# Four seven-product units of eight in the feed-forward input of a macaron trunk, in alternating order

## The chip, the cores and the metric

One core of a Trainium2 chip runs the whole program. The metric is the device time of one execution in microseconds (us). The engines named here: TensorE (PE) with its weight loads (PEld), VectorE (DVE), ScalarE (ACT), GpSimd (POOL), and SyncE (SP), which issues the loads of the weights.

## The reference

A layer of depth one on 256 tokens of width 2048: a SwiGLU block at half weight, an mLSTM mixer, a second SwiGLU block, a final norm.

```python
def swiglu_ffn(x, g, w_in, w_out):
    a, b = jnp.split(rmsnorm(x, g) @ w_in, 2, axis=-1)
    return (jax.nn.silu(a) * b) @ w_out

h = h + 0.5 * swiglu_ffn(h, ffn_norm[0, 0], ffn_w_in[0, 0], ffn_w_out[0, 0])
u = rmsnorm(h, mix_norm[0])
h = h + mlstm_mixer(u, a_w_in[0], a_b_if[0], a_head_norm[0], a_w_out[0])
h = h + 0.5 * swiglu_ffn(h, ffn_norm[0, 1], ffn_w_in[0, 1], ffn_w_out[0, 1])
return rmsnorm(h, final_norm)
```

All arrays are float32; w_in is 2048 x 11264, w_out 5632 x 2048.

## The kernel before

**Precision.** Every wide product is made of three TensorE matmuls of rounded operands: high x high, high x low, low x high. ScalarE writes the high part of a weight tile (a copy into the rounded type), VectorE the low part (raw minus high). So each weight passes through both engines before TensorE reads it. `product` (lines 486 to 490) is one such triple on one 128x512 tile, here called a product.

**The feed-forward input.** The output columns of w_in come in 11 pairs of 512-column tiles, a (left, for silu) and b (right). The first pair is computed the plain way by `run` (line 426). The other ten, `GROUPS` = 10, go through units. A unit takes one pair of k tiles, k and k + 8, and both column tiles: a 2x2 block of weights against a 2x2 block of inputs (two token tiles T0 and T1, two k). Done plainly that is 8 products (`plain_unit`); with sums of inputs (`s_hi`, `s_lo`) and sums of weights (`mixed`) it is 7, after Strassen and Winograd (`seven_unit`). There are 8 units in a group; `UNITS` gives the order plain, seven, plain, seven, plain, seven, plain, plain. The eight products of a plain unit go to the banks p2, p4, p5 and p3, those of a seven unit to p1 to p7. A plain unit uses differences of the inputs (`d_hi`, `d_lo`) for p3.

**Items and slots.** The high and low weights lie in 3 slots each. A plain unit fills one slot (an item), in two halves; a seven unit two: the straight item (three of the raw tiles) and the mixed item (four sums). So a group has 11 items, and item n lies in slot n mod 3. `free` makes ScalarE wait until TensorE has used the item three before (`pair_used`). Raw weights have 3 slots of their own, one for a unit; `load_groups` on the SP queue issues two loads for a unit when the unit three before has been read.

**Queues.** The order on each engine is written out by hand. For one group:

- TensorE: `plain_unit` or `seven_unit` in the order of `UNITS`; after units 1 and 2 `turn_hidden` transposes the hidden tile of the group before.
- ScalarE (`ffn_in` of the scalar block): `high_plain`, `high_straight`, `high_mixed` halves; `silu` of the group before; `keep_hidden` twice; `keep_first`, which copies p1 into `sums`.
- VectorE (`ffn_in` of the vector block): for a seven unit `mix_weights` (three instructions, the later ones waiting for the earlier), `low_straight`, `low_mixed` twice; for a plain unit `low_plain` twice; and the drains of the banks, `drain_products` (p6, p7), `drain_left` (p2, p4), `drain_right` (p5), `drain_last` (p3), then `gate_hidden`.

**The boundary of groups.** The first unit is plain. Its first four products write p2 and p4 and wait for `drain_left` of the group before (`drained`, all but two); the next four write p5 and p3 and wait for all five drains. VectorE does `drain_products` between the two halves of the next group's unit 0, and the other drains behind `mix_weights` and `low_straight` of its unit 1.

**Lines.** 426 matmuls of `run`; 483 hidden transposes; 488 to 490 `product`; 750 and 1139 high and low parts outside the units; 825, 834 and 843 ScalarE's high parts of plain halves, straight and mixed items; 1221, 1229 and 1238 VectorE's low parts of the same; 1253, 1256 and 1258 `mix_weights`; 1266 and 1268 `drain_products`; 1275, 1282 and 1289 left, right and last drain; 1211 `gate_hidden`; 1201 `gate_first`; 1400 `low_hidden`.

Of the kernel before, what the change touches and what calls it, by code (L numbers as in the profile page):

```python
# [5 lines left out]
F32 = mybir.dt.float32  # L6
# [6 lines left out]
P = 128  # L13
# [3 lines left out]
RING = 4  # L17
EPS = 1e-6
UNITS = (("plain", 3), ("seven", 0), ("plain", 4), ("seven", 1), ("plain", 5), ("seven", 2),
         ("plain", 6), ("plain", 7))  # L20
SEVENS, PLAINS = 3, 5
FIRST_ITEM = (0, 1, 3, 4, 6, 7, 9, 10)
ITEMS = 11
# [4 lines left out]
def trunk_program(nc, x, ffn_norm, ffn_w_in, ffn_w_out, mix_norm, a_w_in, a_b_if, a_head_norm,  # L28
# [54 lines left out]
    with ExitStack() as ctx:  # L83
# [16 lines left out]
        gain_rows = sb("gain_rows", [3 * KD, P])  # L100
        first_rows = sb("first_rows", [KD, P])
# [40 lines left out]
        with ExitStack() as side_place:  # L142
            def sp_(name, shape, dt=F32):
                return side_place.enter_context(nc.sbuf_tensor(name, shape, dt))

            sp_("side_pad", [P, KF, SEQ])
            d_sum = sp_("d_sum", [P, 2, PLAINS, P])
            sp_("side_pad2", [P, 25 * SEQ])
            u_all = sp_("u_all", [P, KD, SEQ])
            s_sum = sp_("s_sum", [P, 4, SEVENS, P])  # L150
# [8 lines left out]
        with ExitStack() as gate_place:  # L159
# [7 lines left out]
            select = gp("select", [HEADS, HEADS, P], F32R)  # L167
        with ExitStack() as end_place:
# [3 lines left out]
        ctx.enter_context(nc.sbuf_tensor("place_fence", [P, 98, SEQ], F32))  # L172
# [244 lines left out]
        def _(pe):  # L417
# [76 lines left out]
            def plain_unit(i, group, u, k):  # L494
# [3 lines left out]
                first, last = u == 0, u == len(UNITS) - 1  # L498
                done = DRAINS * (GROUPS * i + group)
                if first and group:  # L500
                    pe.wait_ge(drained, done - 2)
                elif first:
                    pe.wait_ge(silu_ready, SILUS[i] + 1)
                pe.wait_ge(pair_low, halves(i, n) + 1)
                for b, kk in enumerate((k, k + HALF_K)):
                    for bank, tok in ((p2, T0), (p4, T1)):
                        mm = product(bank, u_hi[:, kk, tok], u_lo[:, kk, tok], hi[:, b], lo[:, b],
                                     first and b == 0, last and b == 1)
                mm.then_inc(pair_used, 1)
                if first and group:  # L510
                    pe.wait_ge(drained, done)
                elif first and i == 0:
                    pe.wait_ge(gains_ready, 2)
                pe.wait_ge(pair_low, halves(i, n) + 2)
                for b, kk in enumerate((k, k + HALF_K)):
                    mm = product(p5, u_hi[:, kk, T1], u_lo[:, kk, T1], hi[:, 2 + b], lo[:, 2 + b],
                                 first and b == 0, last and b == 1)
                if last:
                    mm.then_inc(right_summed, 1)
                for b in range(2):  # L520
                    mm = product(p3, d_hi[:, b, k - SEVENS], d_lo[:, b, k - SEVENS], hi[:, 2 + b],
                                 lo[:, 2 + b], first and b == 0, last and b == 1)
                mm.then_inc(pair_used, 1)

            def seven_unit(i, group, u, k):
# [3 lines left out]
                first, last = k == 0, k == SEVENS - 1  # L529
                pe.wait_ge(pair_low, halves(i, n) + 2)  # L530
                product(p1, u_hi[:, k, T0], u_lo[:, k, T0], hi[:, 0], lo[:, 0], first, last)
                product(p2, u_hi[:, k + HALF_K, T0], u_lo[:, k + HALF_K, T0], hi[:, 1], lo[:, 1],
                        False, False).then_inc(pair_used, 1)
                product(p3, s_hi[:, 3, k], s_lo[:, 3, k], hi[:, 2], lo[:, 2], False, False)\
                    .then_inc(pair_used, 1)
                hi, lo = hi_slots[(n + 1) % SLOTS], lo_slots[(n + 1) % SLOTS]
                if first and group == 0:
                    pe.wait_ge(tile_ready, R_HID[i] - R_HID1 + 1)
                pe.wait_ge(pair_low, halves(i, n + 1) + 1)
                product(p5, s_hi[:, 0, k], s_lo[:, 0, k], hi[:, 0], lo[:, 0], False, False)  # L540
                product(p7, s_hi[:, 2, k], s_lo[:, 2, k], hi[:, 1], lo[:, 1], first, last)\
                    .then_inc(pair_used, 1)
                pe.wait_ge(pair_low, halves(i, n + 1) + 2)
                product(p6, s_hi[:, 1, k], s_lo[:, 1, k], hi[:, 2], lo[:, 2], first, last)
                product(p4, u_hi[:, k + HALF_K, T1], u_lo[:, k + HALF_K, T1], hi[:, 3], lo[:, 3],
                        False, False).then_inc(pair_used, 1)

            def ffn_in_rest(i):
# [4 lines left out]
                for group in range(GROUPS):  # L553
                    for u, (kind, k) in enumerate(UNITS):
# [4 lines left out]
                        if u == 1 or u == 2:  # L559
                            turn_hidden(i, group, u - 1)  # L560
# [181 lines left out]
        def _(act):  # L742
# [94 lines left out]
            def high_mixed(i, group, u, half):  # L837

                n, s = item(group, u) + 1, SEVENS * (GROUPS * i + group) + UNITS[u][1]
                act.wait_ge(mixed_ready, 3 * s + (3 if half else 1))  # L840
                free(i, n, half)
                at = slice(2 * half, 2 * half + 2)
                nc.scalar.activation(hi_slots[n % SLOTS][:, at], mixed[:, at], ACT.Copy)\  # L843
# [9 lines left out]
            def keep_first(i, group):  # L853

                act.wait_ge(pair_used, halves(i, item(group, 5)) + 1)
# [14 lines left out]
            def ffn_in(i):  # L870
# [10 lines left out]
                for group in range(GROUPS):  # L881
                    if group == 0:
                        high_plain(i, group, 0, 0)
                        high_plain(i, group, 0, 1)
                    high_straight(i, group, 1)
                    high_mixed(i, group, 1, 0)
                    if group:
                        silu(i, group - 1)
                    high_mixed(i, group, 1, 1)
                    high_plain(i, group, 2, 0)  # L890
                    high_plain(i, group, 2, 1)
                    high_straight(i, group, 3)
                    keep_hidden(i, group, 0)
                    high_mixed(i, group, 3, 0)
                    high_mixed(i, group, 3, 1)
                    high_plain(i, group, 4, 0)
                    high_plain(i, group, 4, 1)
                    keep_hidden(i, group, 1)
                    high_straight(i, group, 5)
                    high_mixed(i, group, 5, 0)  # L900
                    high_mixed(i, group, 5, 1)
                    high_plain(i, group, 6, 0)
                    high_plain(i, group, 6, 1)
                    keep_first(i, group)
                    high_plain(i, group, 7, 0)
                    high_plain(i, group, 7, 1)
                    if group < GROUPS - 1:
                        high_plain(i, group + 1, 0, 0)
# [769 lines left out]
```

## Time and profile before

| | us |
|---|---|
| median of 3 runs | 1840.58 (1840.19 to 1841.08) |
| the profiled execution | 1839.55 |
| its span, first to last instruction | 1837.5 |
| PE busy in the span | 1820.7 (99%), 8228 matmuls |
| DVE busy | 1314.6 (72%) |
| ACT busy | 938.8 (51%) |
| HBM read | 347.24 MB, 190 GB/s over the span |

A busy time is the time in which an engine had an instruction in work, so for TensorE, whose matmuls overlap, it says little more than that it did not wait. The distance between the starts of two instructions is what one costs in a full queue. "Idle before" and the arrow behind it give how long the engine stood still and what released it.

### The profile page before, as it was taken

What the parts mean: (1) busy time and instruction counts of PE and PEld (TensorE: products, weight loads), DVE (VectorE), ACT (ScalarE), POOL (GpSimd) and SP (SyncE); (2) the same over time, 40 slices, a digit from 0 to 9 for tenths busy, and PEclk for the clock granted to TensorE, in tenths of its full rate; (3) what the DMA queues carried; (4) which work ended last, traced back from release to release, by engine and by line L of the source; (5) the groups of instructions that cost most, each with busy time, mean ns of one, the idle gap of its engine ahead of it and who ended that gap; (6) DMA issues with size and microseconds to landing.
All of it is one profiled execution on the core that took longest, in us unless ns stands there. A gap on an engine that the chain in (4) does not pass through costs nothing.

```text
span 1837.5 us, 21636 instructions
## 1 busy us (share of the span) xinstructions
PE 1820.7 (99%) x8228; PEld 1506.1 (82%) x8228; DVE 1314.6 (72%) x1470; ACT 938.8 (51%) x1040; POOL 38.2 (2%) x52
## 2 busy tenths in 40 slices
PE   8999999999999999999999999999999999999998
PEld 6888888888888888888888888888888888888886
DVE  7888888888855554555477757888888888754444
ACT  6555555555654444444445445555555555653442
POOL 0000000000100000000000000000000000000000
PEclk9999999999999999999999999999999999999999
DMA  7666555665556565557645456666665566556664
GB/s 230 222 210 206 196 197 184 197 200 199 178 182 200 190 191 182 166 169 206 192 140 149 160 183 190 211 207 207 204 202 187 184 205 202 194 188 198 194 193 137
DMA packets 180607, 350.68 MB, mean 191 GB/s; under 512 B 10848, under 2 KB 11040, under 8 KB 180256
## 3 DMA queue, kind: packets, MB, share of 16 engines
q1 hardware_dynamic: 179952, 348.17, 59.3%
q0 software_dynamic: 432, 1.18, 0.3%
q8 instruction: 63, 1.03, 0.2%
q14 instruction: 32, 0.26, 0.0%
q10 hardware_dynamic: 128, 0.03, 0.0%
HBM read 347.24 MB, written 2.10 MB: 190 GB/s over the span
## 4 chain that ended last, share of the span: by engine, by line
PE 98%; DVE 1%; ACT 1%; issue 0%; DMA 0%; DVEq 0%; ACTq 0%
PE acc L426 49%; PE acc L490 8%; PE acc L488 8%; PE acc L489 8%; PE aux L490 7%; PE aux L488 7%; PE aux L489 7%; PE aux L483 1%; PE aux L455 1%; PE aux L699 1%; PE aux L649 0%; PE aux L687 0%; DMA h<-in_x_dram 0%; ACT sums L787 0%; ACT u_hi L765 0%
## 5 line engine op out<-in xcount | busy, mean ns | idle before, releaser
L1139 DVE TENSOR_TENSOR w_lo<-raw,w_hi 128x1024 fp32r<-128x1024 f32 x336 | 410.8, 1228 | 330.0 <-ACT w_hi L750 327.5
L750 ACT ACTIVATE w_hi<-raw 128x1024 fp32r<-128x1024 f32 x336 | 354.4, 1059 | 349.7 <-PE acc L426 339.7
L426 PE MATMUL acc<-w_hi,g_hi 128*128 128x512 f32 x704 | 274.9, 390 | 0.0
L426 PE MATMUL acc<-w_hi,g_lo 128*128 128x512 f32 x704 | 274.0, 389 | 0.0
L426 PE MATMUL acc<-w_lo,g_hi 128*128 128x512 f32 x704 | 273.9, 389 | 0.0
L426 PE MATMUL acc<-w_hi,u_hi 128*128 128x512 f32 x512 | 203.9, 398 | 2.8 <-DVE w_lo L1139 2.8
L426 PE MATMUL acc<-w_hi,u_lo 128*128 128x512 f32 x512 | 200.2, 391 | 0.0
L426 PE MATMUL acc<-w_lo,u_hi 128*128 128x512 f32 x512 | 200.2, 391 | 0.0
L1221 DVE TENSOR_TENSOR w_lo<-raw,w_hi 128x1024 fp32r<-128x1024 f32 x112 | 135.2, 1222 | 51.2 <-ACT w_hi L825 51.2
L825 ACT ACTIVATE w_hi<-raw 128x1024 fp32r<-128x1024 f32 x112 | 116.4, 1057 | 87.1 <-PE aux L490 46.1
L426 PEld LDWEIGHTS acc<-w_hi,g_lo 128*128 128x128 f32 x704 | 132.1, 188 | 27.4
L426 PEld LDWEIGHTS acc<-w_lo,g_hi 128*128 128x128 f32 x704 | 132.2, 188 | 27.2
L426 PEld LDWEIGHTS acc<-w_hi,g_hi 128*128 128x128 f32 x704 | 132.2, 188 | 27.3
L488 PE MATMUL acc<-w_hi,u_hi 128*128 128x512 f32 x358 | 140.7, 393 | 0.0
L490 PE MATMUL acc<-w_hi,u_lo 128*128 128x512 f32 x358 | 139.6, 390 | 0.0
L489 PE MATMUL acc<-w_lo,u_hi 128*128 128x512 f32 x358 | 139.4, 389 | 0.0
L426 PEld LDWEIGHTS acc<-w_hi,u_hi 128*128 128x128 f32 x512 | 96.6, 189 | 22.6 <-issue 2.8
L426 PEld LDWEIGHTS acc<-w_hi,u_lo 128*128 128x128 f32 x512 | 96.5, 189 | 20.6
L426 PEld LDWEIGHTS acc<-w_lo,u_hi 128*128 128x128 f32 x512 | 96.7, 189 | 18.9
L1238 DVE TENSOR_TENSOR w_lo<-mixed,w_hi 128x1024 fp32r<-128x1024 f32 x72 | 85.7, 1218 | 1.8 <-ACT w_hi L843 0.2
L843 ACT ACTIVATE w_hi<-mixed 128x1024 fp32r<-128x1024 f32 x72 | 74.5, 1053 | 17.9 <-PE acc L490 17.9
L834 ACT ACTIVATE w_hi<-raw 128x1536 fp32r<-128x1536 f32 x28 | 41.8, 1491 | 75.6 <-PE aux L490 66.8
(227 smaller groups left out, 3231.6 us busy)
## 6 DMA issues: line engine op xcount, KB each, us to landing
raw<-in_ffn_w_in_dram SPq DMA_DIRECT2D x248, 512.0 KB, 4.5
raw<-in_ffn_w_out_dram SPq DMA_DIRECT2D x176, 512.0 KB, 4.6
raw_more<-in_ffn_w_in_dram SPq DMA_DIRECT2D x104, 512.0 KB, 4.5
raw<-in_a_w_in_dram SPq DMA_DIRECT2D x96, 512.0 KB, 4.3
raw<-in_a_w_out_dram SPq DMA_DIRECT2D x32, 512.0 KB, 4.5
h<-in_x_dram SPq DMA_DIRECT2D x4, 512.0 KB, 8.8
final_gain<-in_final_norm_dram POOLq DMA_DIRECT2D x1, 1024.0 KB, 5.3
out_dram<-h SPq DMA_DIRECT2D x1, 1024.0 KB, 3.9
```

Source lines behind the costliest of these rows:

```text
L426: mm = nc.tensor.matmul(acc[:, TT * (c % 2) + t, :], s[:, k, tok], w[:, ring, kk, :], start=(k == 0 and n == 0), stop=(k == GK * granules ...
L455: mm = nc.tensor.transpose(ps[:, at:at + P], block_, ident[:, :])
L488: nc.tensor.matmul(bank, side_hi, wide_hi, start=start, stop=False)
L489: nc.tensor.matmul(bank, side_hi, wide_lo, start=False, stop=False)
L490: return nc.tensor.matmul(bank, side_lo, wide_hi, start=False, stop=stop)
L750: nc.scalar.activation(w_hi[:, n % RING], raw[:, n % RING], ACT.Copy)\
L825: nc.scalar.activation(hi_slots[n % SLOTS][:, at], raw_slots[unit % SLOTS][:, at], ACT.Copy)\
L834: nc.scalar.activation(hi_slots[n % SLOTS][:, 0:3], raw_slots[unit % SLOTS][:, 0:3], ACT.Copy)\
L843: nc.scalar.activation(hi_slots[n % SLOTS][:, at], mixed[:, at], ACT.Copy)\
L1139: nc.vector.tensor_tensor(w_lo[:, n % RING], raw[:, n % RING], w_hi[:, n % RING].bitcast(F32), ALU.subtract)\
L1221: nc.vector.tensor_tensor(lo_slots[n % SLOTS][:, at], raw_slots[unit % SLOTS][:, at], hi_slots[n % SLOTS][:, at].bitcast(F32), ALU.subtract)\
L1238: nc.vector.tensor_tensor(lo_slots[n % SLOTS][:, at], mixed[:, at], hi_slots[n % SLOTS][:, at].bitcast(F32), ALU.subtract)\
```

## The change

Four of the eight k pairs become seven-product units, and the order alternates: seven, plain, seven, plain, and so on. A group has 12 items instead of 11. The first unit of a group is now a seven unit, and its third product (p3) waits for all five drains of the group before. The mixed item is no longer halved in 2 + 2 tiles but in 3 + 1 (`low_mixed`, `low_added`). `drain_products` moves behind `low_straight` of the next group's unit 0. The sums of weights stay on VectorE. The two tiles of raw gains get another place in memory, to make room for the wider `s` tiles.

```diff
-UNITS = (("plain", 3), ("seven", 0), ("plain", 4), ("seven", 1), ("plain", 5), ("seven", 2),
-         ("plain", 6), ("plain", 7))
-SEVENS, PLAINS = 3, 5
-FIRST_ITEM = (0, 1, 3, 4, 6, 7, 9, 10)
-ITEMS = 11
+UNITS = (("seven", 0), ("plain", 4), ("seven", 1), ("plain", 5),
+         ("seven", 2), ("plain", 6), ("seven", 3), ("plain", 7))
+SEVENS, PLAINS = 4, 4
+FIRST_ITEM = (0, 2, 3, 5, 6, 8, 9, 11)
+ITEMS = 12
...
             def seven_unit(i, group, u, k):
...
+                done = DRAINS * (GROUPS * i + group)
+                if first and group:
+                    pe.wait_ge(first_kept, GROUPS * i + group)
+                elif first:
+                    pe.wait_ge(silu_ready, SILUS[i] + 1)
                 pe.wait_ge(pair_low, halves(i, n) + 2)
                 product(p1, u_hi[:, k, T0], u_lo[:, k, T0], hi[:, 0], lo[:, 0], first, last)
+                if first and group:
+                    pe.wait_ge(drained, done - 2)
                 product(p2, u_hi[:, k + HALF_K, T0], u_lo[:, k + HALF_K, T0], hi[:, 1], lo[:, 1],
-                        False, False).then_inc(pair_used, 1)
+                        first, False).then_inc(pair_used, 1)
+                if first and group:
+                    pe.wait_ge(drained, done)
...
+                product(p3, s_hi[:, 3, k], s_lo[:, 3, k], hi[:, 2], lo[:, 2], first, False)\
                     .then_inc(pair_used, 1)
                 hi, lo = hi_slots[(n + 1) % SLOTS], lo_slots[(n + 1) % SLOTS]
+                pe.wait_ge(pair_low, halves(i, n + 1) + 1)
+                product(p5, s_hi[:, 0, k], s_lo[:, 0, k], hi[:, 0], lo[:, 0], first, False)
...
+                product(p7, s_hi[:, 2, k], s_lo[:, 2, k], hi[:, 1], lo[:, 1], first, last)
+                product(p6, s_hi[:, 1, k], s_lo[:, 1, k], hi[:, 2], lo[:, 2], first, last)\
                     .then_inc(pair_used, 1)
                 pe.wait_ge(pair_low, halves(i, n + 1) + 2)
                 product(p4, u_hi[:, k + HALF_K, T1], u_lo[:, k + HALF_K, T1], hi[:, 3], lo[:, 3],
-                        False, False).then_inc(pair_used, 1)
+                        first, False).then_inc(pair_used, 1)
...
-                        if u == 1 or u == 2:
-                            turn_hidden(i, group, u - 1)
+                        if u == 1 or u == 3:
+                            turn_hidden(i, group, u // 2)
...
+            def high_mixed(i, group, u):
...
+                act.wait_ge(mixed_ready, 3 * s + 2)
+                free(i, n, 0 if n >= SLOTS else 1)
+                nc.scalar.activation(hi_slots[n % SLOTS][:, 0:3], mixed[:, 0:3], ACT.Copy)\
+                    .then_inc(pair_high, 1)
+
+            def high_added(i, group, u):
...
+                act.wait_ge(mixed_ready, 3 * s + 3)
+                free(i, n, 1)
+                nc.scalar.activation(hi_slots[n % SLOTS][:, 3], mixed[:, 3], ACT.Copy)\
                     .then_inc(pair_high, 1)
...
                 for group in range(GROUPS):
...
+                    high_straight(i, group, 0)
+                    high_mixed(i, group, 0)
+                    high_added(i, group, 0)
                     if group:
                         silu(i, group - 1)
...
+                    high_plain(i, group, 1, 0)
+                    high_plain(i, group, 1, 1)
...
+                    high_plain(i, group, 5, 0)
                     keep_hidden(i, group, 1)
...
+                    high_plain(i, group, 5, 1)
...
                     high_plain(i, group, 7, 0)
                     high_plain(i, group, 7, 1)
...
+                    keep_first(i, group)
...
             def drain_products(i, group):
...
-                dve.wait_ge(pair_used, halves(i, item(group, 5) + 2))
+                dve.wait_ge(pair_used, halves(i, item(group, 6) + 2) - 1)
...
                 for group in range(GROUPS):
...
+                    mix_weights(i, group, 0)
+                    low_straight(i, group, 0)
                     if group:
+                        drain_products(i, group - 1)
+                        low_mixed(i, group, 0)
                         drain_left(i, group - 1)
...
                         drain_right(i, group - 1)
                         drain_last(i, group - 1)
...
+                        low_added(i, group, 0)
                         gate_hidden(i, group - 1)
                     else:
                         gate_first(i)
...
+                        low_mixed(i, group, 0)
+                        low_added(i, group, 0)
+                    low_plain(i, group, 1)
...
+                    mix_weights(i, group, 6)
+                    low_straight(i, group, 6)
+                    low_mixed(i, group, 6)
+                    low_added(i, group, 6)
+                    low_plain(i, group, 7)
+                drain_products(i, GROUPS - 1)
```

## Rows read from the trace of the kernel before

**Rows 1.** The page, part 1: busy time (share of the span) and instructions.
```profile
PE 1820.7 (99%) x8228; PEld 1506.1 (82%) x8228; DVE 1314.6 (72%) x1470; ACT 938.8 (51%) x1040; POOL 38.2 (2%) x52
```

**Rows 2.** Busy time by stretch: the stage in block one, and one group.
```profile
core 0: us, PE busy (x) PEld busy (x) DVE busy (x) ACT busy (x) POOL busy (x), PEclk, DMA share, GB/s
58.95:483.42 424.47, 424.47 (x1911) 351.35 (x1910) 368.90 (x350) 239.69 (x243) 0.00 (x0) 1.00 0.60 199
101.18:143.62 42.44, 42.44 (x192) 35.14 (x191) 36.99 (x36) 23.68 (x25) 0.00 (x0) 1.00 0.60 199
```

**Rows 3.** Waits of TensorE, whole run: us in total, times, longest us.
```profile
PE acc L426 <- DVE w_lo L1139: 2.8, 2, 2.4
```

**Rows 4.** The chain that ended last: start us, us, what.
```profile
495.42 54.45 PE acc L426 x240
```

**Rows 5.** Timeline of VectorE: start us, us, engine, line, operation, out<-in.
```profile
134.76 0.68 DVE L1266 TENSOR_TENSOR sums<-acc,sums 128x512 f32<-128x512 f32 x1
135.48 0.69 DVE L1268 TENSOR_TENSOR sums<-acc,sums 128x512 f32<-128x512 f32 x1
136.08 1.22 DVE L1221 TENSOR_TENSOR w_lo<-raw,w_hi 128x1024 fp32r<-128x1024 f32 x1
...
140.28 1.76 DVE L1229 TENSOR_TENSOR w_lo_more<-raw_more,w_hi_more 128x1536 fp32r<-128x1536 f32 x1 [0.40 <-ACT w_hi_more L834]
141.96 1.22 DVE L1275 TENSOR_TENSOR tile<-acc,sums 128x1024 f32<-128x1024 f32 x1
143.09 1.21 DVE L1238 TENSOR_TENSOR w_lo<-mixed,w_hi 128x1024 fp32r<-128x1024 f32 x1
144.23 1.21 DVE L1282 TENSOR_TENSOR sums<-aux,sums 128x1024 f32<-128x1024 f32 x1
145.54 0.69 DVE L1289 TENSOR_TENSOR sums<-aux,sums 128x512 f32<-128x512 f32 x1
146.15 1.22 DVE L1238 TENSOR_TENSOR w_lo<-mixed,w_hi 128x1024 fp32r<-128x1024 f32 x1
147.28 1.41 DVE L1211 SCALAR_TENSOR_TENSOR tile<-sums,rstd,tile 128x512 f32<-128x512 f32 x2
148.61 1.22 DVE L1221 TENSOR_TENSOR w_lo<-raw,w_hi 128x1024 fp32r<-128x1024 f32 x1
...
151.78 1.22 DVE L1253 TENSOR_TENSOR mixed<-raw 128x1024 f32<-128x1024 f32 x1
...
154.37 1.75 DVE L1229 TENSOR_TENSOR w_lo_more<-raw,w_hi_more 128x1536 fp32r<-128x1536 f32 x1
```

**Rows 6.** The page, part 6: loads, number, KB each, median us to landing.
```profile
raw<-in_ffn_w_in_dram SPq DMA_DIRECT2D x248, 512.0 KB, 4.5
```

**Rows 7.** Timeline of three engines at one handover.
```profile
106.61 0.39 PE L490 MATMUL aux<-w_hi_more,d_lo 128*128 128x512 f32 x1
...
107.10 1.06 ACT L825 ACTIVATE w_hi_more<-raw 128x1024 fp32r<-128x1024 f32 x1 [1.66 <-PE aux L490]
...
108.19 1.23 DVE L1221 TENSOR_TENSOR w_lo_more<-raw,w_hi_more 128x1024 fp32r<-128x1024 f32 x1 [0.81 <-ACT w_hi_more L825]
```

**Rows 8.** The chain, and TensorE's timeline, where it waited once.
```profile
35.76 1.24 DVE w_lo L1139
...
37.04 0.50 PE L426 MATMUL acc<-w_hi,u_hi 128*128 128x512 f32 x1 [0.40 <-DVE w_lo L1139]
...
37.38 0.40 PE L426 MATMUL acc<-w_lo,u_hi 128*128 128x512 f32 x1
```

**Rows 9.** Timeline of ScalarE: item 1 of the first group.
```profile
59.23 1.49 ACT L834 ACTIVATE w_hi<-raw 128x1536 fp32r<-128x1536 f32 x1 [4.40 <-PE acc L426]
```

**Rows 10.** Timeline of VectorE at the end of the stage, block one.
```profile
480.90 1.23 DVE L1275 TENSOR_TENSOR tile<-acc,sums 128x1024 f32<-128x1024 f32 x1 [0.40 <-PE acc L490]
...
487.37 1.41 DVE L1211 SCALAR_TENSOR_TENSOR tile<-sums,rstd,tile 128x512 f32<-128x512 f32 x2
```

**Rows 11.** Timeline of TensorE at the start of the kernel.
```profile
12.12 0.63 PE L426 MATMUL acc<-w_hi,u_lo 128*128 128x512 f32 x1
12.55 0.63 PE L426 MATMUL acc<-w_hi,u_hi 128*128 128x512 f32 x1
```

## What the change does to the time

> **What bounds the kernel now.** I read the page's busy shares first: TensorE is busy 99% of the span [rows 1]. That view alone can mislead, so next the waits with TensorE as the waiting engine: in the whole run it waits for VectorE twice, 2.8 us together, none of it in the stage that changes [rows 3]. So this is a TensorE-bound kernel, and its time is a count of matmuls times their pitch, 54.45/240 = 0.2269 us [rows 4]. The changed stage runs from 58.95 to 483.42 us and again in the second feed-forward block; there one group takes 42.44 us and in it VectorE is busy 36.99 us [rows 2]. That second number is what to look at: the cover under which the other engines work is 5.45 us per group. The group's 183 matmuls take 41.52 us, its two blocks of transposes the remaining 0.92.
>
> **What is removed.** A plain unit has 8 products of 3 matmuls, a seven-product unit 7. One unit in each of 20 groups changes kind: 60 matmuls x 0.2269 = 13.6 us. If TensorE never waited, a group would take 180 x 0.2269 + 0.92 = 41.76 us.
>
> **What VectorE gets.** I cost its instructions by start-to-start distance where nothing was waited for [rows 5]: a 1024-wide subtraction 1.14 us (143.09 to 144.23), a 1536-wide one 1.68 (140.28 to 141.96), a 512-wide step 0.61 (145.54 to 146.15), the three sums of `mix_weights` together 2.59 (151.78 to 154.37), the two of `drain_products` 1.32 (134.76 to 136.08), a 1024-wide drain whose successor waits for it 1.31 (144.23 to 145.54), `gate_hidden` 1.33 (147.28 to 148.61). After the change a group has 8 plain halves (9.12), 4 x 2.59 of sums (10.36), 8 of the 1536-wide (13.44), 4 of the 512-wide (2.44) and the drains (1.32 + 1.31 + 1.31 + 0.61 + 1.33 = 5.88): 41.24 us against 41.76. The cover is down to half a microsecond, so any wait of VectorE that cannot be made up shows. The loads are not in play: they carry the same bytes and land 4.5 us after their issue [rows 6], and each slot is refilled some ten microseconds before its unit is read. Moving the two gain tiles costs no instruction. ScalarE keeps over a third of its time free and matters only as a link in a chain.
>
> **Where the order decides.** Let X be the time since a group began, for a TensorE that does not stall; a product is 0.68 us. Items end at: 0 at 2.04, 1 at 4.76, 2 at 10.20 (then transposes), 3 at 12.71, 4 at 15.43, 5 at 20.88 (transposes), 6 at 23.39, 7 at 26.11, 8 at 31.56, 9 at 33.60, 10 at 36.32, 11 at 41.76. A slot is refilled when TensorE has used the item three before. How long such a handover takes is in [rows 7]: the last matmul of a half starts at 106.61, so its slot ends at 106.84; ScalarE starts at 107.10, VectorE at 108.19: 0.26, then 1.09.
> Now the new boundary. The next group's third product (into p3) waits for all five drains of the group before, and VectorE does the drains behind `mix_weights(0)`, `low_straight(0)`, `drain_products` and `low_mixed(0)`. It can't begin these before the second half of unit 7 (item 11), whose slot is free when item 8 is used: X = 31.56 + 0.26 + 1.09 = 32.91. I walked the queue up to there: by its own work VectorE would come to that half at about 32.0 (it waits once more, at unit 5, for ScalarE behind the hidden transposes, and still gets there first). Then 1.14 + 2.59 + 1.68 + 1.32 + 1.68 = 8.41, so `drain_left` starts at 41.32. Left, right and last take 1.31 + 1.31 + 0.69, and TensorE goes on 0.04 behind them: that step is 37.04 behind 35.76 + 1.24 in the chain; its next matmul comes 0.34 instead of 0.23 after, 0.11 more [rows 8]. Together 3.46: p3 effectively starts at 44.78. It was due at 41.76 + 1.36 = 43.12. Stall per boundary 1.66 us. In the steady state it is one loop: p3 to the end of item 8, 129 matmuls and two blocks of transposes, 30.20; handover 1.35; VectorE 8.41; drains and restart 3.46; sum 43.42 against 42.44 now. It does not grow, since every part hangs on the stalled TensorE again. There are 9 boundaries in each of two blocks: 18 x 1.66 = 29.9 us.
> p2, due at X = 42.44, waits for `drain_left` (42.54) a tenth of a microsecond, inside the same stall. `low_added(0)` and `gate_hidden` behind the drains are in time: their readers come 2.7 us and more after p3. Before, the first unit after a boundary was plain: four products on p2 and p4, 2.72 us long, covered the right and last drains; the new order has 1.36 us there.
>
> **Start of the stage.** Item 1 of group 0 takes a slot that is free only when the last granule is used; ScalarE starts there at 59.23 now [rows 9], for a unit that TensorE reads 5.44 us into the group. Now it is read at 2.04: 59.23 + 1.49 + 0.04, `low_mixed(0)` 1.75, restart 0.15 gives 62.65 against 58.95 + 2.04 = 60.99: 1.66 us. `gate_first` (59.2 to 60.6) hides under ScalarE's copy. The preparation of the sides gets 0.5 us longer (wider by a third, the differences narrower) in a part where VectorE has time. Twice: 3.3 us.
> **End of the stage.** `drain_products` waits for item 10's first half, X = 35.9; then `low_hidden(0)` behind its copy (37.7) and two splits put `drain_left` at 41.08, its end at 42.30, and TensorE, due at 41.76, goes on at 42.4: 0.7. The gate comes 6.47 after the left drain (487.37 after 480.90 [rows 10]) and ends at 48.96; the transposes are due after 24 matmuls at 47.9: 1.1. Twice 1.8 = 3.6 us.
>
> **Sum.** On the profiled execution, 1839.55 us: - 13.6 + 29.9 + 3.3 + 3.6 = + 23.2, so 1862.8. The median of the runs is 1.0 above the profiled one: 1863.8, and I say 1863.5, since part of the restart may overlap.
> Bounds. The restart at a stall is between 0.04 and 0.15: 2 us over 18. The 512-wide copy on ScalarE and 1536-wide instructions from `mixed` have no row, but have the same shapes' rows and stand off the loop or in it once at 1.68 +- 0.05. Start and end stalls together between 3 and 8 us. That gives 1857 to 1869 for the forecast's own case; nothing excludes small waits more per loop of 0.1 to 0.2, to 1872.
>
> **Rule against row.** TensorE runs at the full one of its levels (2.4 GHz) throughout this stage: granted 1.00 [rows 2]. At the start of the kernel, after idling, the matmuls come 0.43 us apart (12.12, 12.55), 1.2 GHz, for 8 matmuls [rows 11]. The idle of about 0.8 us before 37.04 was followed at once by the full pitch [rows 8]. No row here has a gap of 1.4 us in a busy stretch. The Trainium skill, "TensorE: Matmul & The Clock Gate", section "A second HAM failure mode: psum-queue depth-cycling", says that frequent small idles between groups can make the clock fall and rise again. By that rule the change would lose more than my sum; it is a rival below. No run here shows it yet.
>
> **Rivals.**
> (a) The cover holds, and the time falls. Mechanism: the drains reach p3 in time, that is `drain_left` starts by X = 39.8 instead of 41.32. Then only the matmuls count, and the start and end at their lower bound: 1840.6 - 13.6 + 3 = 1830, or 1827 with none. For it: VectorE's work, 41.24, does fit into 41.76, and at every other reader but this one my walk finds it in time by 0.3 us or more. Against: the handover through item 8 is fixed by TensorE itself and 8.41 us of VectorE's work stand behind it. It decides once that chain is 1.5 us shorter. Chance 0.07.
> (b) The wait at unit 7 is not the last, VectorE's own stream is: the half at 32.02 instead of 32.91, stall 0.77. Then 18 x 0.77 = 13.9, sum + 7.2: 1848. For it: a halving of the handover (the record of PE's ends is modelled). Against: [rows 7] repeats at every plain half. Chance 0.07, and another 0.04 for a mixture of (a) and (b) that ends within 3.7 us of 1840.6.
> (c) The clock falls at each boundary: 8 matmuls at 0.43 instead of 0.23 are 1.6 us, inside the loop, 18 times: + 29, 1892. Chance 0.04.
> (d) The forecast, 1850 to 1872: 0.78.
>
> **Numbers.** A measurement of this kernel can tell about 0.2% (3.7 us) from no change. Faster 0.07 (a); same 0.04; slower 0.89 (forecast, b, c). The range goes from 1847, which takes in (b), to 1872; outside are (a), the mixture and (c), 0.15.
>
> **What would show it.** In the profile after: 8168 matmuls, 60 fewer than the 8228 of now [rows 1]; the waits list gets a new line, TensorE for VectorE's `drain_last` (L490 or L488 on aux, 18 times, about 1.5 us each) and a smaller one for `drain_left`; one group takes 43.4 us; VectorE is busy about 41 us of it, with one wait of 0.9 us for ScalarE before unit 7's second half and one of about 1.3 before unit 5's. The granted clock stays 1.00. I am wrong if `drain_left` starts more than 1.9 us before a group ends, if TensorE waits at another place than p3, or if the distance of groups is under 42.4.

## The result, and the profile after

| | us |
|---|---|
| median after, 4 runs | 1864.87 (1863.99 to 1865.23) |
| before, beside them | 1840.83 |
| ratio, 95% interval | 1.0131 [1.0115, 1.0147] |
| profiled execution after, its span | 1865.09, 1863.0 |
| predicted | 1863.5 (1847 to 1872) |

The kernel became 24 us slower. The 1840.83 is the median of four executions beside it, three of them from 1840.19 to 1841.08 and one, far outside, at 5542.8 us. The page, part 1, against [rows 1]:

```profile
PE 1819.7 (98%) x8168; PEld 1492.3 (80%) x8168; DVE 1391.6 (75%) x1550; ACT 965.2 (52%) x1060; POOL 37.5 (2%) x52
```

The 60 matmuls are gone, but TensorE's busy time fell by 1.0 us and not by 13.6. A record of a matmul lasts 0.39 us at a pitch of 0.23, so the first 0.16 us of each stall counts as busy, and a delay shorter than that does wholly. The busy line hides the loss; the view to read is the waits of TensorE (engine, line, what it waited for: us in total, times, longest us), against [rows 3]:

```profile
PE aux L489 <- DVE sums L1304: 20.9, 18, 1.2
...
PE acc L427 <- DVE w_lo L1146: 2.8, 2, 2.4
PE aux L489 <- DVE w_lo L1245: 2.8, 2, 1.4
PE aux L484 <- DVE tile L1218: 1.8, 2, 0.9
...
PE acc L427 <- DVE tile L1290: 0.9, 2, 0.4
```

The old line (2.8, two times) is still there. New are one wait for `drain_last` (L1304) at each of the 18 boundaries (1.16 us of idle each, where the prediction had said about 1.5), two for `low_mixed` (L1245) at the starts of the stage, and two each for the gate (L1218) and the left drain (L1290) at its ends. The smaller wait for `drain_left`, p2's, is too short for the list of TensorE (0.13 us, all of it counted as busy). The list of the weight loads (PEld) has it, beside the same 18 for `drain_last`:

```profile
PEld aux L489 <- DVE sums L1304: 28.7, 18, 1.6
...
PEld acc L489 <- DVE tile L1290: 7.1, 18, 0.4
```

One group, from left drain to left drain, by stretch (columns as in [rows 2]; there 42.44 us with VectorE busy 36.99):

```profile
189.97:233.45 43.48, 42.32 (x189) 34.41 (x188) 40.76 (x40) 25.06 (x25) 0.00 (x0) 1.00 0.59 194
```

One boundary, VectorE's timeline from the second half of unit 7 on (start us, us, engine, line, operation, out<-in, idle before and what ended it):

```profile
225.06 1.23 DVE L1229 TENSOR_TENSOR w_lo_more<-raw,w_hi_more 128x1024 fp32r<-128x1024 f32 x1 [0.92 <-ACT w_hi_more L828]
...
231.79 1.75 DVE L1245 TENSOR_TENSOR w_lo<-mixed,w_hi 128x1536 fp32r<-128x1536 f32 x1
233.45 1.22 DVE L1290 TENSOR_TENSOR tile<-acc,sums 128x1024 f32<-128x1024 f32 x1
234.77 1.23 DVE L1297 TENSOR_TENSOR sums<-aux,sums 128x1024 f32<-128x1024 f32 x1
236.10 0.69 DVE L1304 TENSOR_TENSOR sums<-aux,sums 128x512 f32<-128x512 f32 x1
```

and TensorE's at the same boundary, p1's first matmul, p2's first, p2's last, p3's first:

```profile
233.91 0.39 PE L489 MATMUL aux<-w_hi,u_hi 128*128 128x512 f32 x1
...
234.72 0.50 PE L489 MATMUL acc<-w_hi,u_hi 128*128 128x512 f32 x1
...
235.30 0.39 PE L491 MATMUL acc<-w_hi,u_lo 128*128 128x512 f32 x1
236.85 0.50 PE L489 MATMUL aux<-w_hi,s_hi 128*128 128x512 f32 x1 [1.16 <-DVE sums L1304]
```

The chain can be read off: VectorE waits 0.92 us for ScalarE, whose slot TensorE has only just given back; then it never pauses until `drain_last`, and TensorE starts p3 0.06 us behind that.

### The profile page after: what moved, and what is told of

Read it like the earlier page. It is cut to its first block, busy times and chain, and to the rows that moved or that the text cites. A ratio compares the mean times of both kernels' runs of the same rounds, so it can differ in the third digit from the quotient of the medians.

```text
span 1863.0 us, 21675 instructions
## 1 busy us (share of the span) xinstructions
PE 1819.7 (98%) x8168; PEld 1492.3 (80%) x8168; DVE 1391.6 (75%) x1550; ACT 965.2 (52%) x1060; POOL 37.5 (2%) x52
## 4 chain that ended last, share of the span: by engine, by line
PE 84%; DVE 10%; issue 4%; ACT 2%; DMA 0%; DVEq 0%; ACTq 0%
PE acc L427 48%; PE acc L489 6%; PE acc L491 6%; PE acc L490 6%; PE aux L489 5%; PE aux L491 5%; PE aux L490 5%; DVE w_lo L1237 2%; DVE sums L1297 1%; DVE tile L1290 1%; DVE mixed L1268 1%; PE aux L484 1%; ACT w_hi_more L828 1%; PE aux L456 1%; DVE sums L1304 1%
## 5 line engine op out<-in xcount | busy, mean ns | idle before, releaser
L1146 DVE TENSOR_TENSOR w_lo<-raw,w_hi 128x1024 fp32r<-128x1024 f32 x336 | 410.6, 1228 | 325.0 <-ACT w_hi L753 322.6
L427 PE MATMUL acc<-w_hi,u_hi 128*128 128x512 f32 x512 | 204.1, 399 | 2.8 <-DVE w_lo L1146 2.8
L427 PE MATMUL acc<-w_hi,u_lo 128*128 128x512 f32 x512 | 200.6, 392 | 0.0
L427 PE MATMUL acc<-w_lo,u_hi 128*128 128x512 f32 x512 | 200.4, 391 | 0.0
L845 ACT ACTIVATE w_hi<-mixed 128x1536 fp32r<-128x1536 f32 x80 | 119.4, 1492 | 138.1 <-DVE mixed L1271 130.4
L1229 DVE TENSOR_TENSOR w_lo_more<-raw,w_hi_more 128x1024 fp32r<-128x1024 f32 x108 | 129.6, 1220 | 28.4 <-ACT w_hi_more L828 28.4
L1245 DVE TENSOR_TENSOR w_lo<-mixed,w_hi 128x1536 fp32r<-128x1536 f32 x80 | 140.0, 1750 | 0.3 <-ACT w_hi L845 0.3
L489 PE MATMUL acc<-w_hi_more,u_hi 128*128 128x512 f32 x320 | 124.5, 389 | 0.0
L490 PE MATMUL acc<-w_lo_more,u_hi 128*128 128x512 f32 x320 | 124.5, 389 | 0.0
L491 PE MATMUL acc<-w_hi_more,u_lo 128*128 128x512 f32 x320 | 124.5, 389 | 0.0
```

The costliest lines, as they stand in the source:

```text
L427: mm = nc.tensor.matmul(acc[:, TT * (c % 2) + t, :], s[:, k, tok], w[:, ring, kk, :], start=(k == 0 and n == 0), stop=(k == GK * granules ...
L489: nc.tensor.matmul(bank, side_hi, wide_hi, start=start, stop=False)
L490: nc.tensor.matmul(bank, side_hi, wide_lo, start=False, stop=False)
L491: return nc.tensor.matmul(bank, side_lo, wide_hi, start=False, stop=stop)
L845: nc.scalar.activation(hi_slots[n % SLOTS][:, 0:3], mixed[:, 0:3], ACT.Copy)\
L1146: nc.vector.tensor_tensor(w_lo[:, n % RING], raw[:, n % RING], w_hi[:, n % RING].bitcast(F32), ALU.subtract)\
```

## The experiments

All are variants of the kernel after, and the edits are shown against it. Each is timed beside the kernel before, whose median was 1839.85 us beside the first four (`extra_unit0` to `drains_first`) and 1840.10 beside the others. A "period" is the distance between two left drains in mid-stage: 42.44 before, 43.48 after, and 41.76 where TensorE never waits. A loop is what runs from one wait of TensorE to the next like it: TensorE's matmuls up to the one that frees a slot, the handover of that slot through ScalarE to VectorE, VectorE's queue up to the result that TensorE waits for, and TensorE's restart (the 0.15 us by which the next two matmuls come late).

**1. More work on the chain.** In groups 1 to 9, ahead of `low_straight` of unit 0, VectorE sums a raw tile into a spare column (declared beside the other tiles) that nobody reads:

```diff
+                if group and u == 0:
+                    nc.vector.tensor_reduce(spare[:, :], raw_slots[unit % SLOTS][:, 0], AXX, ALU.add)
                 nc.vector.tensor_tensor(lo_slots[n % SLOTS][:, 0:3], raw_slots[unit % SLOTS][:, 0:3],
```

> The changed kernel with one more VectorE instruction, a sum over a 128x512 tile whose result nobody reads, ahead of low_straight of unit 0, in 18 of the 20 groups. It stands between the wait for unit 7's second half and drain_left. My theory (a loop through that stretch of the queue, 43.5 us long): all of the instruction's length, about 0.6 us, is added to every group period, 18 x 0.6 = +11, so 1876 against 1864.9. Rival (VectorE's amount of work per group sets the period, wherever it stands): also about +11. This run alone tells nothing, its twin with the same instruction in unit 6 does.

Measured: 1880.14 us (1877.77 to 1881.45), ratio 1.0217 [1.0200, 1.0234]. The period is 44.07 behind all boundaries but 3, + 0.59 for 0.59 us of work: 18 x 0.59 = 10.6, and 1864.9 + 10.6 = 1875.5, as expected. The measured time is 4.6 us above that, which I had not expected. It lies at 3 of the 18 boundaries, where the period is 45.6. There TensorE's timeline, and below it two stretches, read:

```profile
104.55 0.50 PE L490 MATMUL acc<-w_hi,u_hi 128*128 128x512 f32 x1 [0.56 <-DVE tile L1293]
...
106.67 0.51 PE L490 MATMUL aux<-w_hi,s_hi 128*128 128x512 f32 x1 [1.15 <-DVE sums L1307]
107.00 0.60 PE L491 MATMUL aux<-w_lo,s_hi 128*128 128x512 f32 x1
107.40 0.63 PE L492 MATMUL aux<-w_hi,s_lo 128*128 128x512 f32 x1
107.83 0.63 PE L490 MATMUL aux<-w_hi,s_hi 128*128 128x512 f32 x1
```

```profile
104.00:108.00 4.00, 2.31 (x7) 1.59 (x8) 3.79 (x6) 3.23 (x4) 0.00 (x0) 0.88 0.19 74
108.00:112.00 4.00, 4.00 (x14) 3.18 (x13) 3.97 (x5) 1.49 (x1) 0.00 (x0) 0.70 0.04 6
```

Behind the two idles, 0.56 and 1.15 us, TensorE's matmuls come 0.43 us apart, the lower level, with a granted clock of 0.88 and 0.70 in the stretches, until 110.39. From 107.00 to there lie 8 matmuls in 3.39 us instead of 1.82: 1.6 us. That is rival (c) at its price; 3 x 1.6 = 4.7 makes up 1880. At the other 15 boundaries the same two idles left the clock at the full level, and in the kernel after (p2 0.13 late, then 1.16 of idle) it never fell: the granted clock is 1.00 in every 4 us of both stages.

**2. The same work off the chain,** ahead of unit 6 (`u == 6` in place of `u == 0`).

> The same additional instruction, the same number of times, ahead of low_straight of unit 6, where the trace of the changed kernel has VectorE waiting 0.92 us for ScalarE two units later. My theory: it shortens that wait to 0.3 us and costs nothing, 1864.9 within 1.5 us. Rival (the amount of work sets the period): +11, 1876, as in the twin.

Measured: 1864.98 us, ratio 1.0136 [1.0119, 1.0153]; period 43.49. It costs nothing. VectorE's timeline shows where it went, the wait ahead of unit 7's second half, 0.92 before:

```profile
219.00 0.68 DVE L1239 TENSOR_REDUCE spare<-raw 128x1 f32<-128x512 f32 x1
...
225.08 1.23 DVE L1230 TENSOR_TENSOR w_lo_more<-raw,w_hi_more 128x1024 fp32r<-128x1024 f32 x1 [0.33 <-ACT w_hi_more L829]
```

Runs 1 and 2 together: the time hangs on VectorE's work between that handover and `drain_last`, not on its amount in a group.

**3. The readers of the late banks moved back.** TensorE's products of unit 0 (in every group but the first) run in the order p1, p7, p6, p2, p4, p3, p5, those that need no late drain first, and `low_added(0)` goes up:

```diff
+                    pe.wait_ge(drained, done - 3)
...
+                    product(p7, s_hi[:, 2, k], s_lo[:, 2, k], hi_b[:, 1], lo_b[:, 1], True, False)
+                    product(p6, s_hi[:, 1, k], s_lo[:, 1, k], hi_b[:, 2], lo_b[:, 2], True, False)
+                    pe.wait_ge(drained, done - 2)
...
+                    pe.wait_ge(drained, done)
...
                         drain_left(i, group - 1)
+                        low_added(i, group, 0)
                         drain_right(i, group - 1)
                         drain_last(i, group - 1)
-                        low_added(i, group, 0)
```

> The changed kernel with the same work in another order at the boundary: TensorE's seven products of unit 0 run p1, p7, p6, p2, p4, p3, p5 (the two that need no drain of p2 to p5 come early), and VectorE does low_added(0) between drain_left and drain_right. p3 is then due 3.4 us after the boundary instead of 1.36. My theory: drain_last ends at X = 45.07 and p3 is due at 45.17, so the stall of 1.7 us goes, the period is 41.8 and the time 1864.9 - 18 x 1.7 = 1834, up to 1840 if single waits of 0.1 to 0.3 us remain. Rival (amount of work: VectorE needs 41.2 plus its waits of 2.2 us = 43.4): the period stays at 43.4 and the time within 3 us of 1865.

Measured: 1856.96 us (1856.73 to 1858.02), ratio 1.0095 [1.0078, 1.0111]: a miss. The period is 43.07. The wait for `drain_last` is gone, and another stands in its place:

```profile
PE acc L489 <- DVE w_lo_more L1248: 16.8, 18, 0.9
```

It is for `low_plain(1)`, the first half of item 2, next in VectorE's queue behind the drains and the gate. I had checked that reader only in a schedule in which TensorE is already late at p3, not at the period that I now hoped for. Its loop: from TensorE's start of item 2 (X = 4.76) to the end of item 8 (31.56) 26.80; handover 1.35; VectorE 8.41 up to `drain_left`, drains 3.23, `low_added` 0.61, gate 1.33, the half itself 1.22 and restart 0.15, together 14.95: 43.10 against 43.07. By the same walk it was there in the kernel after as well, 0.3 us shorter than the p3 loop of 43.42 and hidden by it.

**4. The drains first,** with TensorE's order left alone:

```diff
                         drain_products(i, group - 1)
-                        low_mixed(i, group, 0)
                         drain_left(i, group - 1)
                         drain_right(i, group - 1)
                         drain_last(i, group - 1)
+                        low_mixed(i, group, 0)
                         low_added(i, group, 0)
```

> The changed kernel with VectorE's order alone changed: low_mixed(0) behind drain_left, drain_right and drain_last instead of ahead of them. Then p3 is in time and p5, which reads the mixed item, is late. By my walk the loop is p5 to the end of item 8 29.52, handover 1.35, VectorE 6.73, left 1.31, right 1.31, last 0.61, low_mixed 1.75, restart 0.15: 42.73 instead of 43.42. That is 18 x 0.69 = -12.4, so 1852.5. Rival (amount of work): 1865. TensorE's wait should move from the drain's sum to the low part of the mixed item, about 1.0 us each.

Measured: 1862.46 us (1862.36 to 1862.85), ratio 1.0123 [1.0107, 1.0140]: a miss again, period 43.37. TensorE now waits for `low_mixed(0)` and, in its weight loads, again for the plain half:

```profile
PE aux L489 <- DVE w_lo L1245: 15.4, 20, 1.4
...
PEld acc L489 <- DVE w_lo_more L1229: 8.0, 18, 0.5
```

Item 2 has the same instructions ahead of it in any order, so its 43.1 remains; its first matmul starts right behind the end of its half in this run too (195.82 behind about 195.77). Of the 0.27 above 43.10, 0.23 is in VectorE's own queue, where `drain_left` now stands directly behind the drain whose sum it reads: 0.83 us from start to start, where the same instruction took 0.60 with another instruction behind it [rows 5].

```profile
186.86 0.69 DVE L1283 TENSOR_TENSOR sums<-acc,sums 128x512 f32<-128x512 f32 x1
187.69 1.23 DVE L1290 TENSOR_TENSOR tile<-acc,sums 128x1024 f32<-128x1024 f32 x1
```

**5. Run 3 with the gate behind item 2.** `gate_hidden` goes behind `low_plain(1)`. VectorE's part, with the edits of run 3 left in on TensorE's side and for `low_added`:

```diff
                         drain_last(i, group - 1)
-                        low_added(i, group, 0)
+                        low_plain(i, group, 1)
                         gate_hidden(i, group - 1)
```

> The run early_mixed came to 1857.0 with a period of 43.07 and a new wait of TensorE for the low part of plain unit 1 (item 2). New theory: p3 was only the first of several readers that VectorE reaches late; the loop through item 2 is TensorE from item 2 to the end of item 8, 26.80, handover 1.35, VectorE 14.94: 43.09. This kernel is early_mixed with gate_hidden moved behind low_plain(1), 1.33 us that item 2 need not wait for. Then item 3 (low_straight of unit 2) is the next late reader: 20.89 + 1.35 + 20.26 = 42.50, so 18 x 0.57 less: 1846.7, and TensorE's wait is at unit 2. Rival (VectorE's amount of work plus waits that don't move, 41.2 + 1.9): the same period 43.1 and 1857.

Measured: 1844.99 us (9 runs, 1844.35 to 1846.13), ratio 1.0027 [1.0017, 1.0037], period 42.40. As forecast, the next reader is late, the straight item of unit 2, whose loop I had walked at 42.50:

```profile
PE aux L489 <- DVE w_lo L1256: 5.8, 18, 0.3
```

So 20 of the 24 us lost come back by order alone, and still the kernel is not faster than before: with VectorE at about 41 us of work in 41.8, each reader has a loop that is a little too long.

**6. Less work on VectorE.** The third sum of each `mix_weights` goes to GpSimd:

```diff
-                dve.wait_ge(mixed_ready, 3 * s + 2)
-                nc.vector.tensor_tensor(mixed[:, 3], src[:, 1], mixed[:, 2], ALU.subtract)\
-                    .then_inc(mixed_ready, 1)
...
+                        pool.wait_ge(mixed_ready, 3 * s + 2)
+                        nc.gpsimd.tensor_tensor(mixed[:, 3], raw_slots[unit % SLOTS][:, 1], mixed[:, 2],
+                                                ALU.subtract).then_inc(mixed_ready, 1)
```

The loads into a raw slot wait for that sum too.

> The changed kernel with the third sum of each mix_weights (128x512, 0.61 to 0.72 us of VectorE) on GpSimd, which is idle in this stage; 4 per group, VectorE's work falls by 2.6 us per group. Loop theory: only the one between unit 7 and drain_left counts, the period goes from 43.48 to 42.8 and the time to 1852.5. Rival 1 (amount): the period is TensorE's own 41.8, 1834. Rival 2 (VectorE and GpSimd hold each other up at the memory): VectorE's instructions beside the sums grow from 1.75 to 2 us or more and the gain is under 6 us.

Measured: 1851.61 us (1851.55 to 1851.87), ratio 1.0063 [1.0046, 1.0080]; period 42.77, that is - 0.71, one sum, for the one sum of four that lies in the loop. Three more sums outside it bought nothing, as run 2 says they should. But VectorE is not 2.6 us freer, by the stretch of one group and by its timeline behind a sum of GpSimd's:

```profile
187.67:230.44 42.77, 42.08 (x189) 34.49 (x189) 41.29 (x37) 25.12 (x25) 10.96 (x4) 1.00 0.60 197
```

```profile
196.98 1.75 DVE L1251 TENSOR_TENSOR w_lo<-raw_more,w_hi 128x1536 fp32r<-128x1536 f32 x1
...
197.15 2.73 POOL L377 TENSOR_TENSOR mixed<-raw_more,mixed 128x512 f32<-128x512 f32 x1 [11.22 <-DVE mixed L1285]
198.65 2.85 DVE L1259 TENSOR_TENSOR w_lo<-mixed,w_hi 128x1536 fp32r<-128x1536 f32 x1
```

Its busy time is 41.29 with four sums fewer, since `low_mixed` beside GpSimd's sum takes 2.85 us instead of 1.75, in units 2, 4 and 6. So VectorE's busy time in a group rose by 0.53 us (40.76 to 41.29) while the period fell by 0.71: once more it isn't the amount of work that sets the period. For the same reason the run doesn't show what less work outside the loop would bring. The section on the hardware returns to this.

**7. The end of the stage alone.** VectorE's order there: one granule is split ahead of the left drain instead of two, the other drains and the gate before the last two:

```diff
                 low_hidden(i, 0)
-                split(g, 0, 2)
+                split(g, 0, 1)
                 drain_left(i, GROUPS - 1)
+                split(g, 1, 2)
                 low_hidden(i, 1)
-                split(g, 2, 3)
                 drain_right(i, GROUPS - 1)
                 drain_last(i, GROUPS - 1)
-                split(g, 3, 4)
                 gate_hidden(i, GROUPS - 1)
+                split(g, 2, 4)
```

> The changed kernel with the new order at the end of the stage alone: drain_left starts at X = 39.94 instead of 41.08, so TensorE finds it done; the gate ends at 46.7, before the transposes are due at 47.9; the third granule is late by 0.2 to 0.3 us. My theory (end term of 1.8 us per block): 3.0 us less, 1861.9. Rival (the end stall only hides another one right behind it): 1864.9 within 1 us.

Measured: 1861.73 us (1861.38 to 1862.23), ratio 1.0118 [1.0102, 1.0135], 3.1 below the kernel after. The waits for the left drain and the gate are gone; a short one for a split is left at each end. Its idle is 0.29 us and its delay 0.47, since that matmul comes 0.88 us behind the start of the transposes (499.28) where it came 0.41 behind it in the kernel after:

```profile
500.16 0.47 PE L427 MATMUL acc<-w_hi,g_hi 128*128 128x512 f32 x1 [0.29 <-DVE w_lo L1146]
```

**8. All three together:** the edits of runs 5, 6 and 7 in one kernel.

> early_late_gate with the third sums on GpSimd and with another order at the end of the stage (VectorE: drain_left ahead of the second granule, the drains and the gate ahead of the third and fourth). By the walk the loop through item 3 is then 42.50 - 2 x 0.7 = 41.1, shorter than TensorE's own 41.76, so no boundary stalls: 1864.9 - 18 x 1.72 - 3 = 1831. Rival (GpSimd's use of the memory slows VectorE): some of the waits stay, 1837 or more.

Measured: 1830.84 us (1830.36 to 1832.28), ratio 0.9951 [0.9934, 0.9967]. It beats both kernels, the one before by 9 us. Of TensorE's waits for VectorE, none is left at a boundary. The first row is the two old waits [rows 3] with the two short ones at the ends of the stage that run 7 left, and the second is the starts of the stage:

```profile
PE acc L441 <- DVE w_lo L1179: 3.4, 4, 2.4
PE aux L503 <- DVE w_lo L1278: 2.8, 2, 1.4
```

```profile
185.74:227.50 41.76, 41.76 (x189) 34.56 (x189) 41.08 (x36) 25.01 (x25) 10.95 (x4) 1.00 0.62 202
```

A group is TensorE's own 41.76 us, and the 34.0 us below the kernel after are 18 x 1.72 = 31.0 and about 3 from the ends. This is the time of rival (a), 1830, with the gain the change could have had.

## Why the prediction was right, and where it was not

The prediction was right in number and in mechanism: the loop that it named is the one that sets the period, and each of its four terms is seen in the trace. Wrong was the condition under which it let rival (a) come true. By term:

- **The matmuls.** 8168, and 41.76 us for a group without waits: run 8's stretch shows that number itself. Right.
- **The boundary.** Predicted was a loop of 43.42 with p3 1.66 us late. Measured: 43.48, 1.72 late, 18 x 1.72 = 31.0 against 29.9. From unit 7's half to `drain_left` it is 225.06 to 233.45, 8.39 against 8.41; left start to last end 3.34 (3.31); restart 0.06 and 0.11 (0.04 and 0.11). Run 1 shows that the loop carries added work one for one, run 2 that work ahead of the handover is free.
- **VectorE's waits** of 0.9 and about 1.3 for ScalarE: 0.92 as shown, and 1.28 ahead of unit 5's. VectorE is busy 40.76 us in a group, against "about 41". The 20 groups' waits of both kinds are one row of the waits:

```profile
DVE w_lo_more L1229 <- ACT w_hi_more L828: 45.2, 40, 1.8
```

- **Start of the stage.** TensorE goes on 1.75 us after the matmul before it instead of 0.23, and its next one is 0.11 late: 1.63 against 1.66. ScalarE starts the mixed item when TensorE gives the slot back, as forecast, and not when the sums are there: they are done at 58.05. No run undid this; it is read from the trace alone.

```profile
60.27 1.49 ACT L845 ACTIVATE w_hi<-mixed 128x1536 fp32r<-128x1536 f32 x1 [3.78 <-PE acc L427]
...
61.85 0.39 PE L491 MATMUL aux<-w_hi,s_lo 128*128 128x512 f32 x1
63.60 0.50 PE L489 MATMUL aux<-w_hi,s_hi 128*128 128x512 f32 x1 [1.37 <-DVE w_lo L1245]
```

- **End of the stage.** 495.40 instead of 494.81 and 0.11 behind: 0.7, as worked out. The transposes at 502.06 instead of 500.98: 1.1. Run 7 leaves a delay of 0.47 twice, so it should take 2.7 of these 3.6 away. The profiled executions differ by 3.7, and 1.0 of that lies at the start of the kernel, see the next point; the medians differ by 3.1.

```profile
494.58 0.39 PE L491 MATMUL aux<-w_hi_more,d_lo 128*128 128x512 f32 x1
495.40 0.50 PE L427 MATMUL acc<-w_hi,g_hi 128*128 128x512 f32 x1 [0.43 <-DVE tile L1290]
...
500.75 0.39 PE L427 MATMUL acc<-w_hi,g_lo 128*128 128x512 f32 x1
502.06 0.66 PE L484 MATMUL aux<-ident,tile 128*128 128x128 f32 x4 [0.92 <-DVE tile L1218]
```

- **The sum.** - 13.6 + 31.0 + 3.3 + 3.6 = + 24.3 for the profiled execution; its time rose by 25.5 (1839.55 to 1865.09). The other 1.1 us are from the kernel's start, ahead of all that changed: in this execution the matmuls came 0.43 us apart for four matmuls more than in the one before, up to the transposes ([rows 11] are from that stretch). The profile's granted clock reads 1.00 there in both kernels, so that column alone would have hidden it; the distance of the matmuls, 0.43 us as in run 1's fall, shows the lower level. The first matmul behind the next transposes stands at 16.24, in the kernel before at 15.13. TensorE's timeline after, and below it before:

```profile
14.74 0.63 PE L427 MATMUL acc<-w_hi,u_lo 128*128 128x512 f32 x1
15.17 1.31 PE L456 MATMUL aux<-ident,h 128*128 128x128 f32 x8
16.24 0.48 PE L427 MATMUL acc<-w_hi,u_hi 128*128 128x512 f32 x1
```

```profile
13.40 0.41 PE L426 MATMUL acc<-w_hi,u_lo 128*128 128x512 f32 x1
...
15.13 0.47 PE L426 MATMUL acc<-w_hi,u_hi 128*128 128x512 f32 x1
```

In the ten profiled executions of this document that matmul stands anywhere from 15.13 to 16.24, in the variants too, so this is no effect of the change. The medians rose by 24.0; how much of the kernel's start is in them, no trace shows.
- **Rival (a), where the walk went wrong.** The prediction let it come true when "the drains reach p3 in time", since "at every other reader but this one my walk finds it in time by 0.3 us or more". That does not hold. I had walked the later readers in a schedule in which TensorE is already 1.66 us late, and the slack that I found there was the stall. Run 3 made the p3 wait vanish, and item 2 was late by 1.3 us; run 5 made that vanish, and item 3 was late. Two of my expectations, for runs 3 and 4, fell on the same error. What (a) needs is all readers in time at a period of 41.76, which run 8 has. The other sentence, "It decides once that chain is 1.5 us shorter", is not refuted by this: no run took 1.5 us of work out of that chain, and since the same 8.41 us stand in the loops of items 2 and 3, an estimate from the walks gives these as 43.10 - 1.5 = 41.6 and 42.50 - 1.5 = 41.0, both below 41.76. By this estimate, moving a reader and removing work are not the same. The forecast was not touched, since for it the stalled schedule is the right one, and its loop was the longest of these.
- **Rivals (b) and (c).** (b) is excluded by the 0.92 us that VectorE still waits ahead of unit 7's half, at every boundary (the row above). (c) did not occur in the kernel after (granted clock 1.00 in the group), but its mechanism and its price are real: run 1 has it at 3 boundaries, 0.6 us of stall further on. I gave it 0.04. The Trainium skill, "TensorE: Matmul & The Clock Gate", section "A second HAM failure mode: psum-queue depth-cycling", describes a kernel in which frequent short idles between groups of matmuls made the clock fall and rise again. The trace of run 1 agrees at 3 boundaries (granted 0.70), and that of the kernel after shows no fall at any of its 18.
- **A misread row.** The prediction calls the gap before 37.04 an "idle of about 0.8 us". The idle in [rows 8] is 0.40; 0.79 us is the distance from the start of the matmul before. Nothing in the sum hangs on it, but the row was weaker evidence on the clock than it was made to be.

What stays open: how much each of run 8's three edits gives in it (only their sum was run), and what decides at which of the 18 equal boundaries of run 1 the clock falls.

## What to carry to other kernels

When one engine's cover shrinks to a few tenths of a microsecond per loop, the busy shares no longer tell the time, the longest loop through its queue does: walk reader by reader around the loop (reader to the slot's release, handover, the queue up to the result). To say what removing the longest loop is worth, compute every loop at the period that you hope for, not in the stalled schedule, where a stall lends slack to all later readers. A stall can be returned only as far as the second-longest loop, and each move of an instruction lengthens the loop of everything that it is moved past.

## What the runs showed of the hardware

**GpSimd and VectorE take turns.** GpSimd's 128x512 sum takes 2713 ns beside VectorE, and 1288 ns at the same size elsewhere in the kernel (the groups of instructions of run 6: line, engine, operation and count, then busy us, mean ns, idle before):

```profile
L377 POOL TENSOR_TENSOR mixed<-raw,mixed 128x512 f32<-128x512 f32 x54 | 146.5, 2713 | 488.3 <-DVE mixed L1285 488.3
...
L425 POOL TENSOR_TENSOR h<-tile,final_gain 128x512 f32<-128x512 f32 x8 | 10.2, 1288 | 233.1 <-DVE tile L1366 177.7 <-DVE tile L1663 55.4
```

In the timeline of run 6 above, GpSimd's sum begins at 197.15, while VectorE's 1536-wide instruction runs until 198.73, and ends at 199.88, 1.15 us after that; the next one of VectorE, from 198.65, ends 1.62 after 199.88. So each seems to have waited for the other's whole instruction, 1.1 us of VectorE's time for each sum moved away, against the 0.7 that the sum costs there. So it is at three of the four sums of a group. At the fourth, in unit 0, the drains of p6 and p7, which read one input from PSUM and one from SBUF, stand beside the sum and keep their 0.68 us, and `low_mixed` its 1.75. The Trainium skill, "SBUF — State Buffer", section "Who interferes with whom", says that a VectorE instruction with two SBUF inputs contends with a GpSimd instruction that reads SBUF, that one with at most one SBUF input (outside VectorE's two-port modes) does not, and that the order of issue decides who blocks. The trace agrees, by the times above. That the loser waits for the whole instruction is the reading of these rows; the section says it only of the two-port modes. The move paid only where the sum was in the loop.

**The clock can fall in a busy stage** behind idles of 0.56 and 1.15 us, as in run 1 at 3 of 18 equal boundaries, for 1.6 us each. Behind a single idle of 1.16 us, in the kernel after, it did so at none of 18.
